# Sixteen latent tokens take gathered key rows in place of dense scores, and the gate blocks are turned by eight

## What is computed

```python
def peer(h, wq, keys, u_tab, v_tab):
    q = (xt @ wq).reshape(T, PEER_HEADS, 2, PEER_DHALF)          # 8 heads, two halves of 128
    s = jnp.einsum('thpd,hpnd->thpn', q, keys)
    v1, i1 = lax.top_k(s[:, :, 0], 16); v2, i2 = lax.top_k(s[:, :, 1], 16)
    ...                                                          # 16 of the 256 pair sums
    e = i1[ci // 16] * 128 + i2[ci % 16]                         # one of 16384 experts
    g = jax.nn.softmax(sc, axis=-1)
    ub = jnp.take(u_tab, eb, axis=0)                             # key rows of 1024
    act = jax.nn.gelu(jnp.einsum('cd,ced->ce', xb, ub))
    vb = jnp.take(v_tab, eb, axis=0)                             # value rows of 1024
    return jnp.einsum('ce,ced->cd', gbk * act, vb)
```

## Time and profile before

| | |
|---|---|
| runs of the kernel before | 2080.81, 2081.55, 2082.29 us |
| median | 2081.55 us |
| the profiled execution | 2080.06 us |
| its span, first to last instruction | 2078.2 us |
| mean granted TensorE clock | 0.987 of 2.4 GHz |
| busy share | PE 97%, DVE 75%, POOL 45%, ACT 44% |
| score stage | 681 to 1422 us |
| values stage | 1422 to 2055 us |

### The profile page before, as it was taken

One profiled execution on the slowest core, in us unless ns is written; L12 is line 12 of the kernel. 1 busy time (PEld: TensorE's weight loads), 2 busy tenths in 40 slices (PEclk: granted clock), 3 DMA queues, 4 the chain that ended last, 5 costly groups with the idle time before them and its releaser, 6 DMA issues.

```text
span 2078.2 us, 34663 instructions
## 1 busy us (share of the span) xinstructions
PE 2013.0 (97%) x11788; PEld 1872.0 (90%) x11788; DVE 1559.3 (75%) x2872; ACT 912.4 (44%) x1508; POOL 926.1 (45%) x652
## 2 busy tenths in 40 slices
PE   4999998999899999999999999999999999999997
PEld 3999998999799999999899999999999999999987
DVE  5559998352479999995666666657888888888887
ACT  3445554222432323233688888863333233332322
POOL 1233332333133477777765666664333333333352
PEclk9999999999899999999999999999999999999997
DMA  9212122434522488888888888779999999999993
GB/s 384 107 61 67 62 60 74 177 122 168 198 62 65 142 302 304 301 306 301 279 333 316 320 330 318 287 251 366 350 346 349 349 344 398 348 344 349 348 361 120
DMA packets 172454, 523.05 MB, mean 252 GB/s; under 512 B 17616, under 2 KB 71248, under 8 KB 170704
## 3 DMA queue, kind: packets, MB, share of 16 engines
q1 hardware_dynamic: 97776, 267.67, 36.7%
q0 software_dynamic: 55296, 201.35, 27.1%
q10 hardware_dynamic: 19296, 52.96, 6.4%
HBM read 463.71 MB, written 58.20 MB: 251 GB/s over the span
## 4 chain that ended last, share of the span: by engine, by line
PE 87%; DMA 5%; DVE 3%; ACT 2%; issue 2%; POOL 1%; SPq 0%; ACTq 0%; DVEq 0%; POOLq 0%
PE P L847 28%; PE P L757 28%; PE P L570 22%; PE P L781 4%; DMA gel_scratch<-gel 2%; PE P L658 1%; DMA rows<-in_v_tab,Eg 1%; PE P L602 1%; PE P L721 1%; DMA tb<-in_posT 1%; DMA raw<-in_wblk 1%; ACT hs L871 1%; ACT hHi L871 1%; PE P L611 0%; PE P L813 0%
## 5 line engine op out<-in xcount | busy, mean ns | idle before, releaser
L871 ACT ACTIVATE wHi<-raw 128x1024 fp32r<-128x1024 f32 x330 | 346.3, 1049 | 1028.7 <-PE P L847 419.0
L512 POOL DMA_INDIRECT rows<-in_v_tab,Eg x192 | 223.6, 1164 | 379.8 <-DVE accB L1711 222.6
L495 POOL TENSOR_TENSOR wLo<-raw,wHi 128x1024 fp32r<-128x1024 f32 x128 | 308.8, 2412 | 182.3 <-ACT wHi L871 179.6
L757 PE MATMUL P<-hHi,wHi 128*128 128x448 f32 x1024 | 380.3, 371 | 3.0 <-POOL wLo L495 3.0
L489 POOL TENSOR_TENSOR wLo<-raw,wHi 128x1024 fp32r<-128x1024 f32 (+1 forms) x76 | 186.1, 2450 | 438.1 <-ACT wHi L871 431.2
L757 PE MATMUL P<-hLo,wHi 128*128 128x448 f32 x1024 | 376.9, 368 | 0.0
L757 PE MATMUL P<-hHi,wLo 128*128 128x448 f32 x1024 | 376.7, 368 | 0.0
L570 PE MATMUL P<-hHi,wHi 128*128 128x320 f32 x960 | 230.1, 321 | 20.2 <-DVE hLo L1300 10.6
L1675 DVE TENSOR_TENSOR pairs<-P,keysel 128x1024 f32<-128x1024 f32 x112 | 132.1, 1220 | 130.4 <-PE P L781 128.1
L570 PE MATMUL P<-hLo,wHi 128*128 128x320 f32 x960 | 221.1, 311 | 0.0
L570 PE MATMUL P<-hHi,wLo 128*128 128x320 f32 x960 | 220.9, 311 | 0.0
(11 more groups left out here) (243 smaller groups left out, 3820.0 us busy)
## 6 DMA issues: line engine op xcount, KB each, us to landing
raw<-in_ublk SPq DMA_DIRECT2D x128, 512.0 KB
raw<-in_v_tab SPq DMA_DIRECT2D x128, 512.0 KB
raw<-in_wblk SPq DMA_DIRECT2D x104, 512.0 KB
gel_scratch<-gel ACTq DMA_DIRECT2D x128, 224.0 KB
gsr<-gel_scratch SPq DMA_DIRECT2D x128, 224.0 KB
gate_scratch<-stage ACTq DMA_DIRECT2D x5, 4096.0 KB, 15.2
gates4a<-gate_scratch SPq DMA_DIRECT2D x16, 640.0 KB
gates4b<-gate_scratch SPq DMA_DIRECT2D x16, 640.0 KB
```

What stands on the lines that cost most here:

```text
L495: pool.tensor_tensor(wLo[:, n % 2, :], raw[:, n % 4, :], wHi[:, n % 2, :].bitcast(f32), ALU.subtract).then_inc(raw_used[n % 4], 1)
L512: pool.indirect_dma_start(out=row(n), out_offset=None, in_=tab, in_offset=bass.IndirectOffsetOnAxis(ap=Eg[:, buf, at:at + 1], axis=0)).the ...
L757: last = nc.tensor.matmul(P[0][:, h, 0:TD], w_[:, h, k * 128:(k + 1) * 128], x_[:, k, C0:T], start=(k == 0 and a == 0 and b == 0), stop=(k ...
L871: return nc.scalar.activation(out, in_, f, **kw)
```

## The change

The latent tokens 64 to 79 (KU = 16) leave the dense score product but stay in the dense values product. Their key rows are gathered: 16 tokens times 128 slots are 16 row blocks of 128 partitions, eight groups of the same 16 tokens. So NU = 208 key gathers stand where NG = 192 were, and `late_rows` spreads 128 rows in place of 112 over the same 62 blocks. The dense product of the scores has 432 columns in place of 448. The gelu tile still has 448 columns; the first 16 are set to 1 once in each buffer, and the gelu of the 16 tokens goes into their softmax weights, from which their gates are made. Since that gelu is known only when the rows 128 to 143 are done, the gate blocks are turned by eight: tokens 64 further on come first, and the chunk with the 16 tokens comes last. The chunks in SBUF are then 0 and 6, no longer 5 and 6.

For the gathers the tokens' activations have to be repeated eight times (`mixH`, VectorE), turned by TensorE, carried by ACT (`accB`, then `htok`) and put where the dots read (`htokP`). The expert numbers are made on the tokens' partitions (`mixE`), moved by a matmul with `mixZ`, masked and reduced. The gelu goes back by a matmul with `tokenM`.

```diff
 def late_rows(b):
-    n, over = NG - D1, U2 - LAG
+    n, over = NU - D1, U2 - LAG
...
+def token_column(b):
+    return C0 + (b + 8) % GB * 8
...
+        def mixed_rows():
+            pe.wait_ge(s["S_ready"], 1)
+            pe.wait_ge(s["mix_h"], 1)
+            for k in range(KC):
+                last = nc.tensor.transpose(P[2][:, k // 4, (k % 4) * 128:(k % 4 + 1) * 128], mixH[:, k, :], ident[:, :])
+            last.then_inc(s["tr_done"], 1)
...
+                if i * 4 + j == 2:
+                    pe.wait_ge(s["htok_ready"], 3)
                 scores(i, j)
+                if i * 4 + j == 1:
+                    mixed_rows()
...
-                        last = nc.tensor.matmul(P[0][:, h, 0:TD], w_[:, h, k * 128:(k + 1) * 128],
-                                                x_[:, k, C0:T], start=(k == 0 and a == 0 and b == 0),
+                        last = nc.tensor.matmul(P[0][:, h, 0:TD - KU], w_[:, h, k * 128:(k + 1) * 128],
+                                                x_[:, k, C0 + KU:T], start=(k == 0 and a == 0 and b == 0),
...
+        pe.wait_ge(s["mix_e"], 1)
+        last = nc.tensor.matmul(P[3][:, 1, MIXC:MIXC + SLOTS],
+                                mixZ[:, :, :].rearrange("p g t -> p (g t)"), mixE[:, :], start=True, stop=True)
         last.then_inc(s["tr2_done"], 1)
...
+        with pe.Fori(0, MIXB // 4 + 1) as i:
+            for j in range(4):
+                expert_scores(i, G0, j)
+                gates_of(i, j)
+        pe.wait_ge(s["mix_w"], 1)
+        nc.tensor.matmul(P[3][:, 0, 0:KU], mixW[:, :, :].rearrange("p g c -> p (g c)"), tokenM[:, :],
+                         start=True, stop=True).then_inc(s["mix_mm"], 1)
+        with pe.Fori(MIXB // 4 + 1, GB // 4) as i:
...
+            elif n == 2:
+                last = actf(accB[:, :].rearrange("p (h n) -> p h n", h=2), P[2][:, :, :], ACT.Copy)
...
+        actf(htok[:, :], accB[:, :], ACT.Copy).then_inc(s["htok_ready"], 1)
...
-            actf(gel[:, h, :], P[0][:, h, 0:TD], ACT.Gelu_apprx_tanh).then_inc(s["gel_free"], 1)
+            if isinstance(i, int) and i * 4 + n0 + j < 2:
+                actf(gel[:, h, 0:KU], ones[:, 0:KU], ACT.Copy)
+            actf(gel[:, h, KU:TD], P[0][:, h, 0:TD - KU], ACT.Gelu_apprx_tanh).then_inc(s["gel_free"], 1)
...
+            if isinstance(ib, int) and ib * 4 + j == GB - 8:
+                act.wait_ge(s["mix_ready"], 1)
...
+            if c == CK:
+                act.wait_ge(s["row_free"], UR + KB)
+                actf(mixG[:, :], actv[:, SLOTS:KB], ACT.Gelu_apprx_tanh).then_inc(s["mix_gelu"], 1)
...
+        V.tensor_copy(mixH[:, :, :].rearrange("p k (g t) -> p k g t", t=KU),
+                      hs[:, :, C0:C0 + KU].unsqueeze(2).broadcast_to([128, KC, 128 // KU, KU])).then_inc(s["mix_h"], 1)
...
+                V.tensor_reduce(tokenM[:, :], ident[:, :].rearrange("p (g t) -> p t g", t=KU), AX.X, ALU.add)
+                V.tensor_copy(mixZ[:, :, :], ident[:, KS:KS + KU].unsqueeze(1).broadcast_to([128, 128 // KU, KU]))
+                V.tensor_reduce(groupM[:, :], ident[:, :].rearrange("p (g t) -> p g t", t=KU), AX.X, ALU.add)
+                V.scalar_tensor_tensor(out=mixE[:, :], in0=keysel[:, 0, TA:TA + SLOTS], scalar=float(NKEY),
+                                       in1=keysel[:, 1, TA:TA + SLOTS], op0=ALU.mult, op1=ALU.add).then_inc(s["mix_e"], 1)
...
+        ch.step(V.tensor_tensor(mixW[:, :, :], P[3][:, 1, MIXC:MIXC + SLOTS].rearrange("p (g c) -> p g c", c=KU),
+                                groupM[:, :].unsqueeze(2).broadcast_to([128, 128 // KU, KU]), ALU.mult))
+        ch.step(V.tensor_reduce(mixG[:, :], mixW[:, :, :].rearrange("p g c -> p c g"), AX.X, ALU.add))
+        V.tensor_copy(E[:, SLOTS:KB], mixG[:, :]).then_inc(s["e_ready"], 1)
...
-                c = C0 + b * 8 + q * 4
+                c = token_column(b) + q * 4
```

95 lines of the change are left out of this document (61 added, 34 removed).

## The result

The kernel before has a median of 2081.18 us (2080.01 to 2082.29), the changed one 2100.74 us (2097.47 to 2104.05): a ratio of 1.0094, 95% interval 1.0078 to 1.011, **slower by 0.9%**. The forecast was 2073.4 us, faster, with a range of 2062 to 2085. The kernel became slower instead, and the time lies 16 us above the range. The profiled execution of the changed kernel took 2101.82 us, its span is 2100.0 us.

A forecast was written before the change was run, and what follows sets the result against it. TensorE's matmuls were taken to bound the kernel, in the second half of the score stage by only 0.3 us; -20.5 + 1.5 + 4.7 + 3.0 + 2.8 + 0.3 = -8.2 us gave 2073.4 us, range 2062 to 2085.

The forecast's parts named there:

- Shorter matmuls, -20.5 us: Score stage on TensorE: 3072 matmuls of 432 columns in place of 448, each 6.7 ns shorter, save 20.5 us.
- Rival C: Score matmul spacing shrinks less than columns do, 1.9 ns for 16 columns; -0.8 us in all, 2080.8 us; chance 0.21.
- TensorE's extras, +1.5 us: After the second score product: eight added transposes, 0.9 us, and two small matmuls, 0.3 us each, on TensorE.
- POOL waits for VectorE, +4.7 us: First half of score stage: POOL's gathers wait for VectorE's dot products, making low halves late for TensorE; costs 4.7 us.
- the sixtieth gather: In block 49, first half: with 3.1 us spare, this gather would be 5.7 us late behind dot 52.
- Rival C's stair of 9 us: Case beside rival C: POOL's first-half waits for VectorE cost 9 us in place of 4.7, giving -3.9 us.
- Gelu stores, +3.0 us: Second half of score stage: gelu stores queue behind 4 MB chunk stores five times, 0.6 us more each; 0.5 to 6.
- The end, +2.8 us: Before block 126: three gathers ahead of POOL's low half make it late for TensorE; 0 to 5 us.
- The switch of row buffers, +0.3 us: Late in the score stage: the switch comes one block later, with the end's waiting pattern, and costs 0.3 us.
- B: All saved columns arrive and nothing waits: -19.0 us, 2062.5 us; chance 0.14.
- D: DMA engines become the bound of the second half of the score stage: slower, 2088.5 us; chance 0.13.
- A: The forecast's own sum of terms, 2073.4 us, own range 2068 to 2079; chance 0.52.

The follow-up runs named there:

- the runs at other widths: Kernel before with score products of 440 or 416 columns in place of 448, omitted tokens not gathered: 2087.99 and 2083.22 us.
- rows alone: Changed kernel with score products of 448 columns again, the first 16 unused, all added work kept: 2095.25 us, ratio 1.0053.
- The shorter blocks alone: Kernel before with score products of 432 columns only, no added gathers or VectorE steps: 2086.39 us, ratio 1.0006.
- the run with two: Changed kernel with late rows counted from the other end, so the last block taking gathers has two, not three: 2089.66 us, ratio 1.0023.
- 64 or 76 rows: Changed kernel with 64 early rows, not 80: 2090.63 us; with 76, later gathers, split stores, late rows from the other end: 2080.05 us.
- the kernel with 64 early rows: Changed kernel with 64 early rows in place of 80, chunk stores split on SP's queue, late rows from the other end: 2070.68 us, ratio 0.9942.

## Why the prediction was wrong

**Shorter matmuls, -20.5 us.** Right in size. 206.67 to 198.90 ns is 7.8 ns, a little above my 6.7 and the slope's 7.5. That both come so near is partly luck: the runs at other widths show steps and no line, and by the line 32 columns would bring 15.0 ns where they bring 20.0. The early blocks fell from 4.96 to 4.77 us (4.80 forecast). With gates the period fell from 6.69 to 6.58, not 6.53. In sum -11.9, -6.3 and -1.3, or -19.5. Rival C is out, and so is the estimate from the Trainium skill's page "TensorE: Matmul & The Clock Gate", section "Back-to-back issue gap", of 2.1 ns for 16 columns; the measurement decides.

**TensorE's extras, +1.5 us.** In line with 684.5 against 683.2 us before the score stage, though single traces with the same program there differ by up to 5.8 us.

**POOL waits for VectorE, +4.7 us. This is the step that failed.** The chain (a gather behind a dot product, the low half behind the gather) was right; its extent was not: the seventeenth gather is already late, and thirteen blocks from 21 to 52 are longer for it, where I had five or six, and the sixtieth gather. The failed sentence is that the dot products "have VectorE's own pace, not TensorE's". With it I moved them by 1.0 us, and the run with rows alone shows about that from the added work (1.7 us at the first dot product, 1.5 at the 68th, the later start of the stage included). But with shorter blocks they are 6.5 us later at the first, 3.4 of it by the later start of the stage, and 20.0 at the 68th. The stair cost 11.9 + 6.1 = 18.0 us (blocks 0 to 63 grew by 6.1), four times the term. I had read the 58.9 of 60 busy microseconds of VectorE in the earlier trace rows as work; some 20 us in 220 of it were waiting under POOL, and the profile books such waiting as busy. Rival C's stair of 9 us was nearer, for no good reason. The term also had a slip: it leaves out that the stage starts 0.9 us later, with which its own working gives 3.8 (the lower bound of 2.9 has it in). Beside 18 us this changes nothing.

**Gelu stores, +3.0 us.** The mechanism was right, the size wrong: the excess of the gate blocks grew by 8.9 us. The shorter blocks alone bring 3.5 and the rows alone 7.2, together more than both in one kernel. ACT's wait grew to 14.6 us where I said 12. What I had left out is TensorE's clock, which fell behind two of the five waits, of 2.57 and 2.04 us (and not behind one of 2.17 us ahead of block 62).

**The end, +2.8 us.** Three gathers ahead of the last low half but one, borne out by the run with two. It cost 5.6 us in these two blocks, double the term: two of the three gathers waited, and the clock fell behind the wait.

**The switch of row buffers, +0.3 us.** Nothing at 80 early rows (block 118 was 7.91 us before and is 8.31 after, block 117 lost its 0.5). With 64 or 76 rows it is 6.9 us; I had not looked at other values.

**The rivals.** B and C are refuted. D named the right side for the wrong reason: the second half moves up to 360 GB/s over 60 us, and 380 in the kernel with 64 early rows, and TensorE waits for no raw block. What is true in it is that the DMA engines are full while a chunk store is in flight. A slower outcome had 0.14, nearly all of it for the one mechanism that didn't come. The mechanism that came was A's own, four times as large. The range took in 2.9 to 6.7 us for a term of which I had priced one direction: VectorE delays POOL. That POOL's low halves delay VectorE, and more so when blocks are short, was left out.

Taken together: -19.5, then +18.0, +8.9, +6.2 (the end's 4.9 and its 1.3 of columns) are 13.6, against 13.8 us measured for the score stage.

## What to carry to other kernels

An engine's busy time may be waiting: before you call a stream independent, compare the longest with the shortest duration of one kind of instruction, and see what ran where it was long. Where two engines wait for each other and one of them is full, price a shorter step elsewhere at nothing or below until spare time is made (here 16 rows moved to the half that had room). And look at what a large store stands in front of in its queue: 4 MB in four pieces on another queue were worth 13.7 us (4.8 in the kernel before) where the whole change could win 19.5.
